# One place size for all expert weight blocks: 14 KB row pieces for the out-weights too, and hidden columns taken as 28p+j

## What is computed

```python
D_MODEL = 1024; N_EXPERTS = 8; TOP_K = 2; EXPERT_DIM = 3584
def swiglu(h, w_in, w_out):                 # w_in (1024, 7168), w_out (3584, 1024)
    g, u = jnp.split(h @ w_in, 2, axis=-1)
    return (jax.nn.silu(g) * u) @ w_out

def moe_swiglu(h, router_w, w_in, w_out):   # combine: softmaxed gates of the two experts of a token
    for e in range(N_EXPERTS):
        out = out + combine[..., e:e + 1] * swiglu(h, w_in[e], w_out[e])
```

## Time and profile before

| | |
|---|---|
| median of 3 runs | 1657.8 us (1656.24 to 1658.26) |
| the profiled execution | 1657.49 us, span of its profile 1655.7 us |
| PE busy | 1565.6 us, 95% of the span |
| DMA in the expert stage from 940 us on | 424 GB/s |

### The profile page before, as it was taken

How to read it: one execution, slowest core, us unless ns; L and a number is a source line. 1 busy time by engine, 2 the same in 40 slices (tenths; PEclk the granted TensorE clock), 3 DMA queues, 4 the chain that set the end, 5 groups by cost and what they waited for, 6 DMA issues and landing times. The chain is left out here.

```text
span 1655.7 us, 27540 instructions
## 1 busy us (share of the span) xinstructions
PE 1565.6 (95%) x12196; PEld 905.3 (55%) x12196; DVE 521.3 (31%) x812; ACT 394.6 (24%) x717; POOL 34.4 (2%) x70
## 2 busy tenths in 40 slices
PE   5999989999999989998899999999999989999887
PEld 2865778878788877866534343343433433334332
DVE  3438377665433366357501001020100201101013
ACT  3338252212222253348401010010100101001011
POOL 1000100010000000000000000000000000000000
PEclk9999999999999999999899999999999999999998
DMA  9762716676524224213698999999999999999995
GB/s 366 218 230 92 228 35 221 202 263 230 195 102 128 96 75 141 82 45 145 241 394 343 414 425 422 424 424 422 425 423 423 423 423 425 423 424 423 423 422 199
DMA packets 87292, 474.34 MB, mean 286 GB/s; under 512 B 9128, under 2 KB 33096, under 8 KB 50304
## 3 DMA queue, kind: packets, MB, share of 16 engines
q1 hardware_dynamic: 84096, 467.64, 71.5%
q0 software_dynamic: 3072, 4.88, 1.1%
HBM read 471.36 MB, written 1.13 MB: 285 GB/s over the span
## 5 line engine op out<-in xcount | busy, mean ns | idle before, releaser
L1192 PE MATMUL ps<-w_moe,h_te 128*32 128x512 f32 (+2 forms) x3776 | 371.1, 540 | 14.9 <-DMA w_moe<-in_expert_in_w_dram 14.9
L1192 PE MATMUL ps<-w_hi,h_t 128*128 128x512 f32 (+1 forms) x960 | 294.7, 388 | 11.7 <-DVE h_t L1876 5.4
L1192 PEld LDWEIGHTS ps<-w_moe,h_te 128*32 128x32 f32 x3776 | 119.6, 110 | 271.7 <-issue 247.8
L1192 PE MATMUL ps<-h_t,w_hi 128*128 128x512 f32 (+1 forms) x768 | 222.1, 374 | 6.2 <-DVE h_t L1876 6.2
L1192 PEld LDWEIGHTS ps<-w_hi,h_t 128*128 128x128 f32 x960 | 180.8, 191 | 49.2 <-issue 4.4
L2343 DVE TENSOR_TENSOR residual<-residual,ps 128x512 f32<-128x512 f32 x24 | 16.5, 688 | 600.0 <-PE ps L1192 600.0
L1818 DVE TENSOR_TENSOR w_lo<-w_raw,w_hi 128x2048 fp32r<-128x2048 f32 x57 | 130.5, 2291 | 228.3 <-ACT w_hi L787 227.8
L1192 PE MATMUL ps<-w_lo,h_t 128*128 128x512 f32 (+1 forms) x480 | 185.3, 386 | 0.0
L787 ACT ACTIVATE w_hi<-w_raw 128x2048 fp32r<-128x2048 f32 x57 | 108.9, 1913 | 302.1 <-PE ps L1192 301.5
L1192 PEld LDWEIGHTS ps<-h_t,w_hi 128*128 128x128 f32 x768 | 140.9, 190 | 33.9 <-issue 9.2
L1192 PE MATMUL ps<-w_moe,work 128*32 128x512 f32 (+1 forms) x1456 | 147.2, 529 | 3.2 <-DVE y_split L2318 3.2
(11 more groups left out here) (281 smaller groups left out, 1125.8 us busy)
## 6 DMA issues: line engine op xcount, KB each, us to landing
w_moe<-in_expert_in_w_dram SPq DMA_DIRECT2D x94, 1792.0 KB, 24.1
w_moe<-in_expert_out_w_dram SPq DMA_DIRECT2D x63, 1024.0 KB, 27.4
work<-in_expert_in_w_dram SPq DMA_DIRECT2D x34, 1792.0 KB, 26.7
w_raw<-in_ada_w_dram SPq DMA_DIRECT2D x48, 1024.0 KB, 5.7
work<-in_expert_out_w_dram SPq DMA_DIRECT2D x30, 1024.0 KB, 26.0
w_raw<-in_ffn_in_w_dram SPq DMA_DIRECT2D x44, 512.0 KB, 5.0
w_extra<-in_expert_out_w_dram SPq DMA_DIRECT2D x19, 1024.0 KB, 27.2
w_raw<-in_diff_qkv_w_dram SPq DMA_DIRECT2D x12, 1024.0 KB, 5.2
```

The costliest lines, as they stand in the source:

```text
L1192: return pe.matmul(out_, l, r, start=first, stop=last, skip_group_check=True)
```

## The change

O blocks become as long as the others. `expert_out_w[e]` is read as 128 partitions of 28 rows (row 28p+j on partition p), which is one contiguous run of 112 KB per partition, and block i takes the i-th eighth of it: 14 KB, three and a half rows, that is seven half rows of 512. There are 8 O blocks of 1.835 MB an expert in place of 14 of 1.049 MB. All places have one size: ten of 14 KB in place of eight of 14 KB and three of 8 KB. The O blocks of expert e stand after every second block of expert e+1 from the fourth on. Since row 28p+j must meet hidden column 28p+j, the columns of the in-blocks are no longer taken as pieces of 512 neighbours, but as four neighbours out of every 28, 128 times; bank 5 takes one out of every 28; and the transposes take every fourth column of a bank. The ahead fetches of O(0,0), O(0,1) and O(0,2) give way to U(0,0) and U(0,1). Some small tiles move to other memory to make room (`SIL5`, `ACT20`, one of the two one-hot tiles, the scratch of `finish`).

```diff
-EB = 2 * DK + ED // 256
+OB = D // P
+ROWS = ED // P
+EB = 2 * DK + OB
@@ first_round
-            order += [b] + ([("O", e, i - LATE)] if i >= LATE else [])
-        order += [("O", e, m) for m in range(2 * DK - LATE, ED // 256)]
-    return order + [("O", NE - 1, m) for m in range(ED // 256)]
+            order += [b] + ([("O", e, (i - LATE) // 2)] if i >= LATE and (i - LATE) % 2 == 0 else [])
+        order.append(("O", e, OB - 1))
+    return order + [("O", NE - 1, m) for m in range(OB)]
-IN_SLOTS, OUT_SLOTS = 8, 3
+SLOTS = 10
@@ first_fetches
-    place = {b: s for s, b in enumerate([b for b in USES if b[0] != "O"][:IN_SLOTS] +
-                                        [b for b in USES if b[0] == "O"][:OUT_SLOTS])}
+    place = {b: s for s, b in enumerate(USES[:SLOTS])}
-        fits = [s for s in free if s < IN_SLOTS or b[0] == "O"]
-        s = min((s for s in fits if s != KEEP or b[1] < NE - 1 or b[0] != "O"), key=lambda s: free[s])
+        s = min((s for s in free if s != KEEP or b[1] < NE - 1 or b[0] != "O"), key=lambda s: free[s])
@@ fetch
-                rows = expert_out_w[0, place, 256 * i:256 * i + 256, :]
-                sp.dma_start(w, rows.rearrange("(p j) n -> p j n", j=2)).then_inc(done, 16)
+                rows = expert_out_w[0, place, :, :].rearrange("(p j) n -> p (j n)", j=ROWS)
+                sp.dma_start(w, rows[:, ED * i:ED * i + ED]).then_inc(done, 16)
@@ experts (SP, first round)
-                fetch(0, "O", 0, 0)
-                fetch(0, "O", 0, 1)
+                fetch(0, "U", 0, 0)
                 sp.wait_ge(hn_done, XT)
-                fetch(0, "O", 0, 2)
+                fetch(0, "U", 0, 1)
@@ in_block
+            w = w.rearrange("p (d j) -> p d j", j=ROWS)
                     if cap == SMALL:
-                        tg, cols = q % 2, w[:, ED // 2 * (q // 2) + 512 * b:ED // 2 * (q // 2) + 512 * b + n]
+                        tg, j = q % 2, ROWS // 2 * (q // 2) + 4 * b
                     elif b == 5:
-                        tg, cols = 2, w[:, 3072 + 256 * (q // 2):3328 + 256 * (q // 2)].rearrange(
-                            "p (d j) -> p j d", j=2)[:, q % 2, :]
+                        tg, j = 2, 24 + q
...
+                    cols = w[:, :, j:j + n // P]
@@ transposes
-                        src = sil(5) if b == 5 else sil(b)[:, 256 * (x // 2):256 * (x // 2) + 256].rearrange(
-                            "p (d j) -> p j d", j=2)[:, x % 2, :]
+                        src = sil(5) if b == 5 else sil(b, BANKS[cap][b]).rearrange(
+                            "p (d j) -> p j d", j=BANKS[cap][b] // P)[:, x, :]
+        def out_half(j, h, w):
+            first, last = j == 0, j == ROWS - 1
+            if h == 0:
                 for tg in range(3):
+                    ins = mm(ps[group(tg), 6, :], hidden(j, tg), w, first, last)
+                return ins
+            mm(ps[group(3), 6, :], hidden(j, 0), w, first, last)
+            for n, (tg, c_) in enumerate(QUARTERS):
+                ins = mm(ps[group(n), 7, 0:256], hidden(j, tg), w[:, 256 * c_:256 * c_ + 256], first, last)
             return ins
+        def out_block(cap, m, w):
+            per = ED // 512
+            for n in range(per):
+                ins = (out_half if cap == CAP else small_out_half)(
+                    (per * m + n) // 2, (per * m + n) % 2, w[:, 512 * n:512 * n + 512])
             return ins
@@ experts (PE), last expert
-                if m == 1:
+                if m == 0:
                     for i in range(4):
                         combine(e - 1, i, i)
-                if m == 3:
+                if m == 1:
```

More of the change, by code:

```diff
@@ L117, in first_fetches @@
 def first_fetches():
-    place = {b: s for s, b in enumerate([b for b in USES if b[0] != "O"][:IN_SLOTS] +
-                                        [b for b in USES if b[0] == "O"][:OUT_SLOTS])}
+    place = {b: s for s, b in enumerate(USES[:SLOTS])}
     free = {s: USE_AT[b] for b, s in place.items()}
-    fills, count, fetches = {b: 1 for b in place}, [1] * (IN_SLOTS + OUT_SLOTS), []
+    fills, count, fetches = {b: 1 for b in place}, [1] * SLOTS, []
     for b in USES:
@@ L292, in sil @@
             return SIL[:, 512 * bank:512 * bank + n]
-        return SIL5[:] if bank == 5 else WMOE[:, (3584, 7680)[bank - 3]:(3584, 7680)[bank - 3] + n]
+        return SIL5 if bank == 5 else WMOE[:, (3584, 7680)[bank - 3]:(3584, 7680)[bank - 3] + n]
     def act_split(part, k):
@@ L362, in backbone @@
     landed = [sem(f"landed{i}") for i in range(RAW)]
-    w_landed = [sem(f"w_landed{i}") for i in range(IN_SLOTS + OUT_SLOTS)]
+    w_landed = [sem(f"w_landed{i}") for i in range(SLOTS)]
     hi_done = sem("hi_done")
@@ L552, in slot_view_moe @@
     def slot_view_moe(s):
[L554 to L561, removed]
+        if s in (2, KEEP):
+            return work(6144 if s == 2 else 2560, ED)
+        at = (8192, 0, None, 4096, None, 11776, 15360, 18944, 22528)
+        return XW[:] if s == SLOTS - 1 else WMOE[:, at[s]:at[s] + ED]
     def nth(kind, i):
@@ L577, in moe_landed @@
             return 16 * FILLS[kind, e, i]
-        each, turn = (ED // 256 // LATER_OUT, i // LATER_OUT) if kind == "O" else \
-            (2 * DK // LATER_IN, nth(kind, i) // LATER_IN)
+        each, turn = (OB // len(LATER_OUT), i // len(LATER_OUT)) if kind == "O" else \
+            (2 * DK // len(LATER_IN), nth(kind, i) // len(LATER_IN))
         return 16 * (FILLED[moe_slot(rnd, kind, e, i)] + (rnd - 1) * NE * each + turn + 1) + e * (16 * each)
@@ L682, in experts @@
                         sp.wait_ge(used, moe_base(rnd) + e * EB +
[L683 removed]
+                                   (n - ins + 1 if n >= ins else 2 * DK - ins + n + 1 - EB))
                         fetch(rnd, kind, e, i)
[L685 removed]
+                for i in range(OB):
                     n = nth("O", i)
                     sp.wait_ge(used, moe_base(rnd) + e * EB +
[L688 removed]
+                               (n - outs + 1 if i >= outs else n - outs + 1 - 2 * DK))
                     fetch(rnd, "O", e, i)
@@ L1635, in out_block @@
[L1635 to L1639, removed]
-                for tg in range(3):
[L1641 to L1645, removed]
-            return ins
@@ L1648, in small_out_block, with hidden @@
[L1648 to L1654, removed]
-                    ins = mm(ps[group(n), 6, :], small_hidden(m, j, tg), w[:, j, 512 * c_:512 * c_ + 512],
-                             first, last)
+        def hidden(j, tg):
+            if j < 20:
+                return ACTT[:, P * j + 32 * tg:P * j + 32 * tg + GROUP]
+            if tg == 2 and j >= 24:
+                return ACT20[:, 32 * (j - 24):32 * (j - 24) + GROUP]
+            at = P * (4 * (tg + 3 * ((j - 20) // 4)) + j % 4) + 96
+            return ACTT[:, at:at + GROUP]
@@ L1657, in small_out_block, with small_out_half @@
+        def small_out_half(j, h, w):
+            for tg in range(2):
+                ins = mm(ps[group(2 * h + tg), 6, :], small_hidden(j, tg), w, j == 0, j == ROWS - 1)
+            return ins
+        def out_block(cap, m, w):
[3 more added lines that the diff above has]
+                    (per * m + n) // 2, (per * m + n) % 2, w[:, 512 * n:512 * n + 512])
             return ins
@@ L1714, in product @@
                         pe.wait_ge(actt_bank, 6 * g + 6)
-                    return (out_block if cap == CAP else small_out_block)(i, weights(kind, e, i)).then_inc(used, 1)
+                    return out_block(cap, i, weights(kind, e, i)).then_inc(used, 1)
                 def hold(b):
@@ L1741, in experts @@
                     transposes(e)
-                    for m in range(ED // 256):
+                    for m in range(OB):
                         product("O", e, m)
@@ L1770, in experts @@
                         pe.wait_ge(acc_done, 4 * e + 1)
-                    product("O", e, i - LATE)
-                for m in range(2 * DK - LATE, ED // 256):
-                    product("O", e, m)
+                    if (i - LATE) % 2 == 0:
+                        product("O", e, (i - LATE) // 2)
+                product("O", e, OB - 1)
             e = NE - 1
```

55 lines of the change are left out of this document (22 added, 33 removed).

## The result

The changed kernel takes 1662.4 us (median of 8 runs, 1660.4 to 1666.0) where the kernel before took 1656.9 beside it: ratio 1.0036, 95% interval 1.002 to 1.0051. It is slower, by some 5 us, and what happened is rival C: PE became slower on strided operands, and used up the cover. The profiled execution takes 1660.65 us, span 1658.8.

The account below looks back on a forecast made before the run. PE bounds expert 0 and the end, the DMA the stretch from 903 to 1597.52 us. From the profiled 1657.5: - 3.8 + 1.5 + 0.9 - 0.6 = -2.0, so 1655.5 us; range 1651 to 1662.

Parts of the forecast that it names:

- rival C: In-blocks and transposes: PE becomes slower on strided operands; 1660.7 us, or 1665 with the other experts counted; chance 0.14.
- the cover: Expert stage: PE's 21.7 us of waits on weight transfers, under which added PE work would be hidden.
- Step 4: Strided reads on PE: 0.9 us for expert 0's transposes (stationary), 0 for the in-blocks' moving operand.
- Step 3: End of the order: U(7,7) lands 3.7 us earlier, PE's larger blocks before the last transposes cost 5.2; together +1.5 us.
- the prediction's own signs: Wrong if expert 0 takes longer than 73 us; in-blocks at 4.7 us instead of 4.52 mean PE slower on strided operands.
- Step 1: Drained queue between experts 0 and 1: 1.31 MB more in the places and less waiting for places; gain 3.8 us.
- Step 2: Ahead fetches: U(0,0) and U(0,1) bring 1.57 MB more between 800 and 825 us, in a nearly empty window; cost 0.
- Step 5: DMA rate with O rows of 14 KB instead of 8 KB: gain 0.6 us, at most 2.8.
- D: O transfers: the wide pitch of 112 KB lowers the DMA's rate; 1663 us at 3%; chance 0.08.
- E: Queue after expert 0: the places don't bring what the plan says; 1659.9 us; chance 0.08.
- Rival B: DMA: longer rows help, 2.8 us for the rate and 4.4 for the drained queue, strided reads free; 1651.8 us; chance 0.18.
- The tail: End of the kernel: PE's last stretch of 30.27 us was to stay as it was.

Follow-up runs that it names:

- e2: The kernel before with only its in-blocks' columns read as 28p+j, O blocks kept; 1661.1 us, ratio 1.0027.
- e6_pairs_flat: The changed kernel with O blocks used two by two and in-blocks' columns read as neighbours; 1652.7 us, ratio 0.9973 to the kernel before.
- e7_flat: The changed kernel with in-blocks' columns read as neighbours, O blocks one by one; 1652.9 us, ratio 0.9968 to the kernel before.
- e8: The kernel before with only the 512-column pieces of the in-blocks read as 28p+j (runs of four floats); 1657.2 us, ratio 0.999.
- f1: The kernel before, only 512-column pieces read as 28p+j, the small experts' second half beginning at j = 16 instead of 14; 1657.6 us, ratio 1.0003.
- e1: The changed kernel with bank 5 of the big experts reading 128 neighbouring floats; 1652.1 us, ratio 0.9967 to the kernel before.
- e3: The changed kernel with O blocks used two by two, after every fourth in-block; 1658.1 us, ratio 1.0008 to the kernel before.

## Why the prediction was wrong

**Step 4, the moving operand, is the step that failed.** It took 0 for the strided reads, where e2's stretches show 3 x 3.89 + 4 x 2.91 = 23 us of PE's time, and expert 0 another 3.6. Step 3 took the new cut of the O blocks at nothing too ("O blocks are cut otherwise"); it is the rest, 3 to 4 us, of the 27.2 by which the stretches of the change grew (3 x 4.43 + 4 x 3.47). Two of the prediction's own signs came: expert 0 took 76.85 us, longer than 73 (73.24 before, so the bound stood close), and a big in-block 4.76, which it put down to C.

The row that step 4 took as the nearest had a stride of two; the change goes to a stride of 28, so to one float of each line, and that is another case: 277 against 405 ns. "Four floats are one line" holds in the big experts; in the small ones' second half the runs lie across two, and that is 2.05 us a stretch. The one sentence that pointed to the single floats was that of the Trainium skill (SBUF — State Buffer, Specifications: two hits on each line for full bandwidth); it was held against the loads of the transposes (141 against 209 ns). Those are of the other operand, and it doesn't behave alike. Here the loads now, min, median and max:

```profile
L1690 PEld LDWEIGHTS ps<-ident,residual x96: 196/209/218, 895.4 to 1608.5; 128*128 128x128 f32 x96
```

So the stationary part of step 4 cost 0, not 0.9: from two floats of a line to one nothing is added. For the moving operand it is the reverse. In bank 5 two hits are nearly free (277 and 280 ns against 273), as the Trainium skill (SBUF — State Buffer, Specifications) has it, and one costs (405). The runs of four across two lines have two hits on each of them and cost all the same (606 to 627 ns against 592), and the runs of two in the small experts cost 395 against 379; there the measurement decides.

**Rival C** named the mechanism, with 0.14. Its price of 0.21 us for a big in-block's single floats stands against 0.245 measured (3.93 / 16), and its 3.4 us for expert 0 against 3.6. Its sum of 30.8 us fits better than its reasons. Measured, with the later stretches taken as the first: 3.6 + 3 x 4.43 + 4 x 3.47 = 30.8. But its 4 x 2.7 + 4 x 1.6 for transposes were nothing; in their place stand the small experts' misplaced runs of four (8), runs of two (4) and the cut of O (3 to 4).

**The cover** was a little wider than the 21.7 us of waits. Where PE has no such waits, a later small stretch is some 2.4 us longer than the first (the change: 96.66 and 94.27; e6_pairs_flat, whose first is that of before: 93.35). By that those of before would take 93.2 without the DMA; they take 96.28, 105.10 and 105.11, 26.9 more in all. That is an estimate; a block after a wait takes 3.21 us alone where it takes 3.02 in a row. 27.2 us of work against 26.9 of cover left the way from the first transposes to the last at 712.36 us, where it was 712.15. (Both sums come from the same stretches, so that they meet so closely is no test of its own.) The profile's span is 3.1 us longer: 3.6 in expert 0, 0.2 on that way and 2.0 in the tail, less 2.7 by which its expert 0 begins earlier. The medians are 5.4 apart; how far the other runs share this start and this tail is not shown. What the change did not win is the forecast's gain.

**Step 1** was right. SP still issues nothing for ten us after expert 0 (10.45 before):

```profile
894.68 0.33 SPq L639 DMA_DIRECT2D w_moe<-in_expert_in_w_dram  x1
904.42 0.34 SPq L636 DMA_DIRECT2D w_moe<-in_expert_out_w_dram  x1
```

From 906 to 940 the rate is 421, over the 415 that was asked for. The sizes of the DMA packets in the traces, added up from the start of the span, give 167.6 MB landed at 903.5 us against 166.3 before, which is the 1.31 MB more in the places, and at 940 us 181.9 (182.3 in e7_flat) against 180.5: 1.4 and 1.8 MB, 3.4 and 4.2 us at 424, against 3.8 taken for the step. In the changed kernel it buys nothing, since PE is late.

**Step 2** was right: the U blocks came in the empty window (268 GB/s against 12), and nobody waits for them.

**Step 3** was right where the queue sets the pace, in e7_flat: wait for O(6,6) 1.08 us (1.3 forecast), transposes 13.9 us after U(7,7) (13.5), 5.4 to the first O block (5.4), and 31.0 to the end (30.27). U(7,7) begins at 1586.4, 3 us ahead of the 1589.4 of steps 1, 3 and 5; most of this is step 5. In the changed kernel itself PE comes there late: its transposes begin at 1606.92.

**Step 5** had the right sign and too small a size. The rounded rates, 425 against 424, hide it; the packets landed from 940 to 1590 us add up to 276.5 MB in each of the ten kernels with the new O blocks and to 275.3 or 275.4 in each of the four with the old (before, e2, e8, f1): 425.4 against 423.6 GB/s. The 1.2 MB are 2.8 us, the upper bound of the step, where 0.6 was taken. Row length, block size and the places change together, so which of them brings it is not shown.

Rivals D and E are out with it: no rate fell, and the places brought what the plan said. Rival B's 2.8 us for the rate came, and of its 4.4 for step 1 up to 4.2, but step 4 hid both. e7_flat, which is the forecast without step 4, came at 1652.9 us, where the sum without its 0.9 was 1654.6 and B 1651.8.

**The tail**, taken as unchanged, is 2 us longer in the change's profile (32.27 against 30.27). The two windows 1612 to 1620, before and after, show the clock:

```profile
1612.00:1620.00 8.00, 8.00 (x52) 2.95 (x48) 2.68 (x4) 0.00 (x0) 0.00 (x0) 0.79 1.01 406
```

```profile
1612.00:1620.00 8.00, 7.70 (x34) 2.43 (x35) 0.88 (x3) 0.00 (x0) 0.00 (x0) 0.62 0.93 394
```

The mean falls after PE's wait for DVE: some of each window is at the lower level (1.2 GHz), and more of it in the change. In e1 and e3 the clock was 1.00 in every window of 4 us from 1600 to 1624, and the same chain took 29.41 us. So the 2 us follow the clock and not PE's work in the tail. The ten profiles with the order of the change have 29.41 to 32.27 us, the four with the old order 29.97 to 31.42; whether the new order keeps PE longer at the lower level is not shown. The gather's gain of 1.5 us at the start is the clock's too.

## What to carry to other kernels

Before a layout is changed, write down for each matmul how many neighbouring floats the moving operand takes and at which multiple of four it begins: four floats that begin at a multiple of four were free here, two cost 3 to 4% of their piece (273 to 280 and 379 to 395 ns), one float half as much again (273 to 405 ns), and four that begin two past a multiple of four 4% of a small block. Price the moving and the stationary operand apart, each from a row of its own kind. And a cover of waits is a budget that all edits share: a cost "hidden under the DMA" is free only until the sum of such costs exceeds it, and on a stretch that belongs to PE (expert 0 here) none of it is hidden. Finally, a rate that is rounded to 1 GB/s can hide the size of a step: here 1.8 GB/s over 650 us were 2.8 us.

## What was not expected of the hardware

- Where a run of four floats begins decides its cost: 3.21 us a small in-block aligned, 3.34 across a multiple of 16 bytes, with equal matmuls; the two column groups that read the misplaced half pay alone (606 to 627 ns against 592).
- The stationary operand is indifferent between every second and every fourth float (209 ns both), though neighbours load in 141; in the same transposes of the kernel before, the last bank, which lies as neighbours, loads in 151.
- An O block that ends in the middle of a row costs PE half a us in each stretch, with every matmul kept. Pairs take it away; the cause within the array wasn't looked for.
- With the misplaced runs the column groups run out of step: in e8 an instruction on the next block's tile starts while the last bank of the block before is still to come. In f1 the same blocks follow each other in clean rows. That the groups do so is seen; that it costs something of its own is not shown.

```profile
905.52 0.60 PE L1193 MATMUL ps<-work,h_te 128*32 128x512 f32 x2
905.54 0.39 PE L1193 MATMUL ps<-w_moe,h_te 128*32 128x256 f32 x2
```

- With O blocks of 14 KB rows in ten equal places the queue moved 425.4 GB/s, with the old ones 423.6 to 423.7, in every profile.
